# Between the scan and the experts: which engine copies the affinities out, who scales token tile eight, where the choice rounds stand, and 48 identity transposes

## The chip, the cores and the metric

The kernel runs on one core of one Trainium2 chip. The core has five engines that work in parallel, each through its own instruction list, and that wait for each other by semaphores: TensorE (PE, matmuls), VectorE (DVE), ScalarE (ACT), GpSimd (POOL) and SyncE (SP, which here only issues DMAs). The metric is the device time of one launch in microseconds (us), lower is better. One launch computes the whole model step for both inputs.

## The reference

Two inputs, a prompt of 256 tokens and a sample of 1024 tokens, of width 1024, go through one layer: a mixer (gated short convolution beside a bidirectional mLSTM) and a mixture of 16 experts in which each expert chooses its tokens. The part that matters here:

```python
def expert_choice_sublayer(x, norm_g, w_router, w_gate, w_up, w_down):
    n_tok = bsz * s
    cap = CAPACITY_FACTOR * n_tok // N_EXPERTS      # 128 for the sample, 32 for the prompt
    tokens = rms_norm(x, norm_g).reshape(n_tok, d)
    logits = jnp.einsum('nd,de->ne', tokens, w_router)
    affinity = jax.nn.softmax(logits, axis=-1)
    gate, idx = lax.top_k(affinity.T, cap)
    xe = tokens[idx]
    hid = jax.nn.silu(jnp.einsum('ecd,edf->ecf', xe, w_gate)) * jnp.einsum('ecd,edf->ecf', xe, w_up)
    ye = jnp.einsum('ecf,efd->ecd', hid, w_down) * gate[..., None]
    out = jnp.zeros((n_tok, d)).at[idx.reshape(-1)].add(ye.reshape(-1, d))
    return x + out.reshape(bsz, s, d)
```

So no expert can start before all affinities of a sequence are known, the top 128 of 1024 tokens have been found for each expert, and those tokens have been gathered.

## The kernel before

**The stages.** Tokens are cut into ten tiles of 128: tiles 0 to 7 are the sample (NS = 8), tiles 8 and 9 the prompt. The kernel first projects all tokens (to about 410 us), then runs a loop over the ten tiles (the scan with the output projection, the residual and the router), then chooses tokens, then runs 16 experts one after the other, then normalises and stores. Every engine's list is written out by hand in the source, so the order of the work on an engine is the order of the calls.

**The tile loop.** All engines run it with a counter n from 0 to NT + 1 = 11. Tile n's heads are computed at step n, its residual x1 (`residual`, L1307, in two halves of 512 columns) at step n + 1, and what is left of it at step n + 2, where m = n - 2 counts the tile: sum of squares (ACT, `token_squares`), router logits (PE, `logits`), softmax (`softmax_terms` on ACT, `affinities` on DVE). The normalised tokens go to DRAM as `tok_d`, from which the experts gather. For tiles 0 to 7 DVE makes them in one operation (`tokens_out`, L1436), and GpSimd issues the DMA. For the two prompt tiles ACT scales (L1042), GpSimd multiplies by the gain (L715) and issues the DMA (L718), after the loop. "Tile eight" in the list of changes is the last sample tile, m = 7.

**The choice.** `choose` (L1297) finds eight tokens a round for all experts together: a MAX8, a FIND_INDEX8 and a MATCH_REPLACE8 over 512 columns. There are 16 rounds, 0 to 15. AFF, the table that they search, is filled from PSUM: the sample's affinities in two copies by DVE (L1543) at step 9, the prompt's after round 11 (L1568). Rounds 0 to 5 lie between the work of the last steps of the loop, rounds 6 to 15 behind it. Then DVE computes the indices (`GIF`, L1584), PE transposes them (L1909), DVE writes `IDX` (L1593), and GpSimd starts two gathers: `xg` for the sample's rows (L743) and `xgp` for the prompt's quarter rows (L746). Both add to one semaphore, `gath`.

**The barrier.** Behind the loop SP, PE, ACT and GpSimd each do `barrier` (L341: `eng.drain().then_inc(bar)`, then wait for all five; DVE only arrives with `arrive` and waits for it before `IDX`). GpSimd first waits until all `acc_d` and `tok_d` writes have landed. Only behind the barrier does SP load expert weights: `load_weights` (L563), 1 MB at a time into `eraw`.

**The first expert.** ACT rounds five weight blocks (`high(0, 0, 0, j)` for j = 0 to 4, L1055, `ehi`), then the gathered tokens (`tokens_high`, L1066, `xc`) and then makes `xb` (`narrow_tokens`, L1061), in this order in its list. DVE makes the low parts (`elo`, `xc`). PE's `token_columns` (L1921) transposes the gathered rows; the expert's first matmul (L1928) waits for `xc`, `xb` and the first weights.

Of the kernel before, what the change touches and what calls it, by code (L numbers as in the profile page):

```python
# [6 lines left out]
ACT = mybir.ActivationFunctionType  # L7
# [6 lines left out]
P = 128  # L14
# [27 lines left out]
def hybrid_conv_mlstm_moe(nc, x_prompt, x_sample, norm1_g, w_in, conv_w, gate_bias, head_norm_g, w_out,  # L42
# [5 lines left out]
    NT = T // P  # L48
# [97 lines left out]
    with out:  # L146
# [157 lines left out]
        def final_tile(n):  # L304
# [18 lines left out]
            "x1_out0 x1_out1 sum2 tk_done tk_out0 tk_out1 xT_ps2 xT_done "  # L323
            "lg_ps lgmax exps aff_done affT_ps topk selT_ps sel_done "

            "er0 er1 er2 er3 er4 er5 er6 er7 ehi elo idx_cp gath exT_ps xc_hi xc_lo xb_done "
            "gu_ps gu_add sg_done hid_done hc_hi hc_lo hb_bf dn_ps y_done scat settled "

            "conv_done cvl_done g2b_in tk_scaled issued gf_in f_in0 f_in1 f_in2 f_in3 f_in4 f_sum f_y f_out f_gath f_same f_row f_sq f_quart f_done f_set").split()}
        x_in = (S["x_in0"], S["x_in1"], S["x_in2"])  # L330

        w_ind, stg = (S["w_in0"], S["w_in1"]), (S["st0"], S["st1"], S["st2"], S["st3"])
# [48 lines left out]
        def joint(m):  # L381

            return m >= NS


        def colslot(c, q):
# [217 lines left out]
        def _(pool):  # L604
# [94 lines left out]
            for n in range(NT + 2):  # L699
                if n >= 2:  # L700
                    m = n - 2
                    t = tokens_of(m)
                    pool.wait_ge(S["x1_done"], 2 * (m + 1))
                    pool.dma_start(acc_d[t, :], d["x1"][:, m % 2, :]).then_inc(x1_out[m % 2], 16)
                if 1 <= n < NT - 1:
                    scale_queries(n + 1)
                if 1 <= n < NT - 2:
                    select_causal(n + 2)
                if n >= 2 and not joint(m):
                    pool.wait_ge(S["tk_done"], m + 1)  # L710
                    pool.dma_start(tok_d[t, :], d["tk"][:, m % 2, :]).then_inc(tk_out[m % 2], 16)
            pool.wait_ge(S["g2b_in"], 16)
            for m in range(NS, NT):
                pool.wait_ge(S["tk_scaled"], m - NS + 1)
                pool.tensor_tensor(d["tk"][:, m % 2, :], d["tk"][:, m % 2, :], g2b, ALU.mult  # L715
                                   ).then_inc(S["tk_done"], 1)
                pool.wait_ge(S["tk_done"], m + 1)
                pool.dma_start(tok_d[tokens_of(m), :], d["tk"][:, m % 2, :]).then_inc(tk_out[m % 2], 16)  # L718
# [21 lines left out]
            def gather(idx):  # L740

                settle()
                pool.indirect_dma_start(f["xg"][:, :], None, tok_d,  # L743
                                        bass.IndirectOffsetOnAxis(ap=idx[:, 0:1], axis=0)
                                        ).then_inc(S["gath"], 16)
                pool.indirect_dma_start(f["xgp"][:, :], None, tok_quarters,  # L746
                                        bass.IndirectOffsetOnAxis(ap=idx[:, 1:2], axis=0)
                                        ).then_inc(S["gath"], 16)

            def scatter(e):  # L750

# [64 lines left out]
        def _(act):  # L816
# [165 lines left out]
            def token_squares(m):  # L982

                act.wait_ge(S["x1_done"], 2 * (m + 1))
                if m >= 1:
                    act.wait_ge(S["sum2"], m)
                act.activation(d["junk"][:, :], d["x1"][:, m % 2, :], ACT.Square, scale=D ** -0.5,
                               accum_out=d["ms"][:, m % 2, 0, H:H + 1]).then_inc(S["sum2"], 1)

            def softmax_terms(m):  # L990

                act.wait_ge(S["lgmax"], m + 1)
                act.activation(aff[:, m, :], psum[:, logit_bank(m), 0:NE], ACT.Exp, bias=logit_max[:, m, 0:1],
                               scale=d["ms"][:, m % 2, 1, H:H + 1],
                               accum_out=logit_max[:, m, 1:2]).then_inc(S["exps"], 1)
# [5 lines left out]
            for n in range(NT + 2):  # L1001
# [31 lines left out]
                    exponentials(n + 2)  # L1033
                if 1 <= n <= NT:
                    columns_out(n - 1, 0)
                if n < NT:
                    heads_high(n)
            for m in range(NS, NT):
                softmax_terms(m)
            for m in range(NS, NT):  # L1040
                act.wait_ge(tk_out[m % 2], 16 * (m // 2))
                act.activation(d["tk"][:, m % 2, :], d["x1"][:, m % 2, :], ACT.Copy, scale=d["ms"][:, m % 2, 1, H:H + 1]  # L1042
                               ).then_inc(S["tk_scaled"], 1)
            barrier(act, 1)

            def high(e, s, h3, j, first=False):
# [96 lines left out]
        def _(dve):  # L1143
# [162 lines left out]
            def residual(n, h):  # L1306
                dve.wait_ge(S["o_ps"], 2 * n + h + 1)  # L1307
                if h == 0:
                    dve.wait_ge(ld_x[n % 2], 16 * (n // 2 + 1))
                    if n >= 2:  # L1310
                        dve.wait_ge(x1_out[n % 2], 16 * (n // 2))
                        dve.wait_ge(S["tk_done"], n - 1)
                    else:

                        for q in range(NST):
                            dve.wait_ge(stg[q], 16 * len([g for g in staged if stage_no[g] % NST == q]))
                dve.tensor_tensor(d["x1"][:, n % 2, 512 * h:512 * h + 512], psum[:, 6 + h, :],
                                  d["xs"][:, n % 2, 512 * h:512 * h + 512], ALU.add).then_inc(S["x1_done"], 1)
# [197 lines left out]
            for n in range(NT + 2):  # L1516
                s, m = n % 2, n - 2
                if n == NT:
                    choose(both_halves, half, CAPS, 0, 2)
                if 1 <= n < NT:  # L1520
                    denominators(n)
                    if n == 1:
# [15 lines left out]
                    affinities(m)  # L1538
                if n == NT - 1:

                    dve.wait_ge(S["affT_ps"], 1)
                    for i in range(NS // 4):
                        ch(dve.tensor_copy(AFF[HALF2 * i:HALF2 * i + NE, :], psum[0:NE, (0, 4)[i], :]))  # L1543
                if n == NT:
                    logit_peak(m)
                    choose(both_halves, half, CAPS, 2, 4)
                if 2 <= n < NT - 1:
                    tokens_out(m)
                if 1 <= n <= NT:
                    residual(n - 1, 1)  # L1550
                if 1 <= n < NT:
                    heads_low(n)
                if n == NT - 1:
                    tokens_out(m)
                if n == NT + 1:
                    choose(both_halves, half, CAPS, 4, 5)
                    last_roots()
                    logit_bias(m - 1)
                    logit_peak(m)
                    logit_bias(m)  # L1560
                    choose(both_halves, half, CAPS, 5, 6)
                    affinities(m - 1)
                    affinities(m)

            arrive(dve)
            choose(both_halves, half, CAPS, 6, 12)
            dve.wait_ge(S["affT_ps"], 2)
            ch(dve.tensor_copy(AFF[PROMPT:SEL, 0:SP_], psum[0:NE, 1, 0:SP_]))  # L1568
            choose(slice(0, SEL), half, CAPS, 12, CAPS // 8)
# [121 lines left out]
        def _(pe):  # L1691
# [218 lines left out]
            pe.wait_ge(S["topk"], 2)  # L1910
            pe.transpose(psum[:, 4, 0:SEL], GV[:, :], ident[0:SEL, 0:SEL]).then_inc(S["selT_ps"], 1)

            def token_columns(e, g, bank):

                pe.wait_ge(S["gath"], 32 * e + 32)
                if bank == TOKEN_BANK:
                    pe.wait_ge(S["xc_lo"], 3 * e + g)
                rows = [f["xg"][:, k * P:(k + 1) * P] for k in range(4 * g, 4 * g + 4)] if g < 2 else \
                       [f["xgp"][:, c * P:(c + 1) * P] for c in range(2)]
                for k, x in enumerate(rows):  # L1920
                    tr = pe.transpose(psum[:, bank, k * P:(k + 1) * P], x, ident[:, :])  # L1921
                tr.then_inc(S["exT_ps"], 1)
# [128 lines left out]
```

## Time and profile before

| | us |
|---|---|
| median of three runs | 1375.62 |
| lowest and highest of the three | 1372.38, 1375.68 |
| the profiled execution, device time | 1374.1 |
| the profiled execution, first to last instruction (span) | 1372.4 |
| PE busy | 1276.9 (93%) |
| DVE busy | 916.6 (67%) |
| ACT busy | 706.2 (51%) |
| POOL busy | 310.5 (23%) |

The profile tells of one execution. Times in its rows count from the span's start. The stretch that the change touches runs from 560 to 660 us. In the page's 40 slices of 34.3 us PE is nearly full everywhere but in slices 18 and 19 (597 to 651 us or so), and there the clock granted to PE stands at 0.7 and 0.5 of full speed.

```profile
PE   4899999999998999943999999999999999999992
PEclk9999999999999999975999999999999999999996
```

### The profile page before, as it was taken

The page shows a single profiled execution, that of the slowest core. Times are in us where ns is not written, and L with a number is a line of the kernel's source. Part 1 is how long each engine was busy: PE and PEld are TensorE (multiplying, and loading weights), DVE is VectorE, ACT ScalarE, POOL GpSimd, SP SyncE. Part 2 cuts the span into 40 slices and gives each one's busy share as a digit, 9 for nine tenths or more (in the row PEclk, how much of TensorE's full clock was granted, in tenths as well). Part 3 has the DMA queues.
Part 4 walks back from the last instruction along what each step waited for, and adds up shares of the span by engine and source line. Part 5 has one row for each costly group of instructions (what it writes and reads, how often), then busy time and mean ns, then how long its engine had stood idle before and what let it go on. Part 6 is the DMA issues. An engine that isn't in the chain of part 4 may idle for free.

```text
span 1372.4 us, 24856 instructions
## 1 busy us (share of the span) xinstructions
PE 1276.9 (93%) x9696; PEld 1111.7 (81%) x9696; DVE 916.6 (67%) x1336; ACT 706.2 (51%) x1025; POOL 310.5 (23%) x304
## 2 busy tenths in 40 slices
PE   4899999999998999943999999999999999999992
PEld 4789999888887888832898889888898888888881
DVE  5345122251377555587888898888888898888976
ACT  5335321101145444314766677667766777666762
POOL 1032222010032232022123313132222313133040
PEclk9999999999999999975999999999999999999996
DMA  7113165314148765119799999999999999999994
GB/s 255 47 39 113 45 208 170 122 60 122 62 131 261 206 199 175 52 77 315 271 336 311 307 317 321 330 306 315 318 331 315 298 316 328 331 309 307 296 363 190
DMA packets 242030, 314.74 MB, mean 229 GB/s; under 512 B 16096, under 2 KB 206048, under 8 KB 241968
## 3 DMA queue, kind: packets, MB, share of 16 engines
q1 hardware_dynamic: 226576, 268.54, 59.4%
q0 software_dynamic: 15392, 45.36, 11.2%
q8 instruction: 41, 0.67, 0.2%
q14 instruction: 21, 0.17, 0.0%
HBM read 274.41 MB, written 39.44 MB: 229 GB/s over the span
## 4 chain that ended last, share of the span: by engine, by line
PE 89%; DVE 6%; DMA 2%; ACT 1%; issue 1%; SPq 0%; POOL 0%; DVEq 0%; ACTq 0%; POOLq 0%
PE psum L1851 25%; PE psum L1928 22%; PE psum L1935 10%; PE psum L1951 8%; PE psum L1743 7%; PE psum L1969 4%; PE psum L1960 4%; PE psum L1921 1%; PE psum L1789 1%; PE psum L1790 1%; PE psum L1776 1%; PE psum L1762 1%; DMA woraw<-in_w_out_dram 1%; PE psum L1724 1%; PE psum L1699 1%
## 5 line engine op out<-in xcount | busy, mean ns | idle before, releaser
L1602 DVE TENSOR_TENSOR elo<-eraw,ehi 128x2048 bf16<-128x2048 f32 x192 | 433.1, 2282 | 1.0 <-POOLq L761 1.0
L1055 ACT ACTIVATE ehi<-eraw 128x2048 fp32r<-128x2048 f32 x192 | 362.3, 1902 | 47.0 <-DMA eraw<-in_w_gate_dram 26.2
L1928 PE MATMUL psum<-xc,ehi 128*128 128x320 f32 x2048 | 332.4, 314 | 1.9 <-DVE xc L1607 1.9
L1928 PEld LDWEIGHTS psum<-xc,ehi 128*128 128x128 f32 x2048 | 304.2, 189 | 3.5 <-DVE xc L1607 2.3
L1935 PE MATMUL psum<-xb,elo 128*128 128x160 bf16 x2048 | 164.6, 234 | 0.0
L1615 DVE TENSOR_REDUCE gu<-psum 128x320 f32<-128x640 f32 x128 | 105.0, 820 | 85.1 <-PE psum L1935 84.9
L1935 PEld LDWEIGHTS psum<-xb,elo 128*128 128x128 bf16 x2048 | 139.3, 98 | 13.2 <-issue 0.2
L1851 PE MATMUL psum<-hn_hi,whi 128*128 128x512 f32 (+1 forms) x384 | 138.1, 360 | 5.8 <-DVE wlo L1179 5.8
L1851 PE MATMUL psum<-hn_lo,whi 128*128 128x512 f32 (+1 forms) x384 | 136.6, 356 | 0.0
L1851 PE MATMUL psum<-hn_hi,wlo 128*128 128x512 f32 (+1 forms) x384 | 136.5, 355 | 0.0
L1951 PE MATMUL psum<-ehi,hc 128*128 128x512 f32 x512 | 132.6, 406 | 0.0
L1951 PEld LDWEIGHTS psum<-ehi,hc 128*128 128x128 f32 x512 | 95.1, 188 | 22.2
L1106 ACT ACTIVATE sg<-gu 128x320 f32<-128x320 f32 x64 | 30.2, 472 | 145.1 <-DVE gu L1615 145.1
L1179 DVE SCALAR_TENSOR_TENSOR wlo<-wraw,g1c,whi 128x256 fp32r<-128x256 f32 x96 | 39.0, 477 | 95.2 <-ACT whi L838 95.1
L1851 PE MATMUL psum<-whi,hn_hi 128*128 128x256 f32 x320 | 91.6, 286 | 0.0
L1851 PE MATMUL psum<-wlo,hn_hi 128*128 128x256 f32 x320 | 90.5, 283 | 0.0
L1851 PE MATMUL psum<-whi,hn_lo 128*128 128x256 f32 x320 | 90.5, 283 | 0.0
L1851 PEld LDWEIGHTS psum<-hn_hi,whi 128*128 128x128 f32 x384 | 73.3, 191 | 16.6 <-DVE wlo L1179 6.0
L1851 PEld LDWEIGHTS psum<-hn_hi,wlo 128*128 128x128 f32 x384 | 73.2, 191 | 10.1
L1851 PEld LDWEIGHTS psum<-hn_lo,whi 128*128 128x128 f32 x384 | 73.3, 191 | 9.6
L754 POOL DMA_INDIRECT acc_d<-yt,idx x15 | 24.1, 1606 | 219.8 <-ACT yp L1076 219.8
L838 ACT ACTIVATE whi<-wraw,g1c 128x256 fp32r<-128x256 f32 x96 | 39.6, 497 | 53.5 <-PE psum L1851 51.5
(251 smaller groups left out, 1971.6 us busy)
## 6 DMA issues: line engine op xcount, KB each, us to landing
eraw<-in_w_gate_dram SPq DMA_DIRECT2D x64, 1024.0 KB, 9.6
eraw<-in_w_up_dram SPq DMA_DIRECT2D x64, 1024.0 KB, 9.9
eraw<-in_w_down_dram SPq DMA_DIRECT2D x64, 1024.0 KB, 13.9
wraw<-in_w_in_dram SPq DMA_DIRECT2D x12, 1024.0 KB, 7.6
negm<-negm_d SPq DMA_DIRECT2D x10, 512.0 KB, 7.4
acc_d<-x POOLq DMA_DIRECT2D x10, 512.0 KB, 5.4
tok_d<-tk POOLq DMA_DIRECT2D x10, 512.0 KB, 2.9
v<-v_d SPq DMA_DIRECT2D x18, 256.0 KB, 4.0
```

The source lines that it names most:

```text
L838: w = act.activation(b["whi"][:, j % 2, k, :], b["wraw"][:, j % 2, k, :], ACT.Copy, scale=b["g1c"][:, k:k + 1])
L1055: act.activation(f["ehi"][:, j % RING, :], f["eraw"][:, raw_slot(s, j), :], ACT.Copy).then_inc(S["ehi"], 1)
L1179: w = dve.scalar_tensor_tensor(b["wlo"][:, j % 2, k, :], b["wraw"][:, j % 2, k, :], b["g1c"][:, k:k + 1], b["whi"][:, j % 2, k, :].bitcast ...
L1602: dve.tensor_tensor(f["elo"][:, j % RING, :], f["eraw"][:, raw_slot(s, j), :], f["ehi"][:, j % RING, :].bitcast(F32), ALU.subtract).then_i ...
L1615: dve.tensor_reduce(f["gu"][:, (i // 2) % 2, i % 2, :, :], both, AX_X, ALU.add).then_inc(S["gu_add"], 1)
L1743: mm = pe.matmul(psum[:, 6 + h, :], x, w, start=(k == 0 and a == 0), stop=(k == KD - 1 and a == 2))
L1851: mm = pe.matmul(o, lhs, rhs, start=(k == 0 and a == 0), stop=(k == KD - 1 and a == 2))
L1928: pe.matmul(o[:, 0:2 * NC], hi[:, k, c], x[:, k, :, :].rearrange("p a t -> p (a t)"), start=(k == 0), stop=False, skip_group_check=True)
L1935: mm = pe.matmul(o[:, NC:2 * NC], lo[:, k, c], xb[:, k, :], start=False, stop=(k == KD - 1), skip_group_check=True)
L1951: mm = pe.matmul(psum[:, 4 + h, :], f["hc"][:, 2 * q + kk, a, :], f["ehi"][:, j % RING, full_columns(kk, h)], start=(q == 0 and kk == 0 an ...
L1960: pe.matmul(psum[:, 4 + h, :], f["hbf"][:, 2 * q + kk, :], f["elo"][:, j % RING, full_columns(kk, h)], start=False, stop=False, skip_group ...
L1969: mm = pe.matmul(psum[CAPP * i:CAPP * (i + 1), 6, 0:CH], f["hid"][:, k, CAPS:NC], f["eraw"][:, raw_slot(s, j), c], start=(k == 0), stop=(k ...
```

## The change

Six edits, all between tile step 9 and the first expert:

1. The sample's affinities are copied from PSUM into AFF by ACT (two ACTIVATE, behind `columns_out` of step 9), no more by DVE.
2. LATE = NS - 1 = 7: tile 7's tokens are treated as those of the prompt tiles. DVE's `tokens_out(7)` is gone; ACT scales the tile in step 9, behind `heads_high`, and GpSimd multiplies by the gain and issues the DMA behind the loop, so that it now does this for three tiles.
3. GpSimd waits for `aff_done` of all ten tiles before the first of these three multiplications.
4. The choice rounds are laid anew: round 0 stands in step 9 ahead of the second half of residual 8, round 1 at the head of step 10, rounds 2 to 4 behind the first half of residual 9, round 5 and 6 in step 11, and rounds 7 to 15 behind the loop.
5. The gather of the prompt's rows has a semaphore of its own, `gath_p`; PE's transposes of the sample's rows wait for `gath` alone.
6. PE does 48 transposes of the identity into a PSUM bank that nobody reads, between the transposes of the choice and those of the gathered tokens.

```diff
+        LATE = NS - 1
@@ GpSimd
-                if n >= 2 and not joint(m):
+                if n >= 2 and m < LATE:
                     pool.wait_ge(S["tk_done"], m + 1)
                     pool.dma_start(tok_d[t, :], d["tk"][:, m % 2, :]).then_inc(tk_out[m % 2], 16)
             pool.wait_ge(S["g2b_in"], 16)
-            for m in range(NS, NT):
-                pool.wait_ge(S["tk_scaled"], m - NS + 1)
+            pool.wait_ge(S["aff_done"], NT)
+            for m in range(LATE, NT):
+                pool.wait_ge(S["tk_scaled"], m - LATE + 1)
                 pool.tensor_tensor(d["tk"][:, m % 2, :], d["tk"][:, m % 2, :], g2b, ALU.mult
                                    ).then_inc(S["tk_done"], 1)
...
                 pool.indirect_dma_start(f["xgp"][:, :], None, tok_quarters,
                                         bass.IndirectOffsetOnAxis(ap=idx[:, 1:2], axis=0)
-                                        ).then_inc(S["gath"], 16)
+                                        ).then_inc(S["gath_p"], 16)
@@ ACT
+            def scaled_tokens(m):
+                act.wait_ge(tk_out[m % 2], 16 * (m // 2))
+                if not joint(m):
+                    act.wait_ge(S["lgmax"], m + 1)
+                act.activation(d["tk"][:, m % 2, :], d["x1"][:, m % 2, :], ACT.Copy, scale=d["ms"][:, m % 2, 1, H:H + 1]
+                               ).then_inc(S["tk_scaled"], 1)
...
+                if n == NT - 1:
+                    act.wait_ge(S["affT_ps"], 1)
+                    for i in range(NS // 4):
+                        act.activation(AFF[HALF2 * i:HALF2 * i + NE, :], psum[0:NE, (0, 4)[i], :], ACT.Copy
+                                       ).then_inc(S["aff_out"], 1)
                 if n < NT:
                     heads_high(n)
+                if n == NT - 1:
+                    scaled_tokens(LATE)
@@ DVE
-                        dve.wait_ge(S["tk_done"], n - 1)
+                        if n - 2 < LATE:
+                            dve.wait_ge(S["tk_done"], n - 1)
+                        else:
+                            dve.wait_ge(S["tk_scaled"], 1)
...
                 if n == NT:
-                    choose(both_halves, half, CAPS, 0, 2)
+                    choose(both_halves, half, CAPS, 1, 2)
...
-                    dve.wait_ge(S["affT_ps"], 1)
-                    for i in range(NS // 4):
-                        ch(dve.tensor_copy(AFF[HALF2 * i:HALF2 * i + NE, :], psum[0:NE, (0, 4)[i], :]))
+                    dve.wait_ge(S["aff_out"], NS // 4)
+                    choose(both_halves, half, CAPS, 0, 1)
                 if n == NT:
                     logit_peak(m)
-                    choose(both_halves, half, CAPS, 2, 4)
+                    choose(both_halves, half, CAPS, 2, 5)
...
-                if n == NT - 1:
-                    tokens_out(m)
                 if n == NT + 1:
-                    choose(both_halves, half, CAPS, 4, 5)
+                    choose(both_halves, half, CAPS, 5, 6)
...
-                    choose(both_halves, half, CAPS, 5, 6)
+                    choose(both_halves, half, CAPS, 6, 7)
...
-            choose(both_halves, half, CAPS, 6, 12)
+            choose(both_halves, half, CAPS, 7, 12)
@@ PE
+            for _ in range(48):
+                pe.transpose(psum[:, 2, 0:P], ident[:, :], ident[:, :])
...
-                pe.wait_ge(S["gath"], 32 * e + 32)
+                if g < 2:
+                    pe.wait_ge(S["gath"], 16 * e + 16)
+                else:
+                    pe.wait_ge(S["gath_p"], 16 * e + 16)
```

GpSimd's list at the end of the tile loop, from the last `tok_d` write inside the loop to the first gather. In the names `x` is a residual tile, `tk` a normalised tile, `og` the gain. Before:

```order
L711 DMA tok_d<-tk 128x1024 [waits s_tk_done]
L704 DMA acc_d<-x 128x1024 [waits s_x1_done] x2
L715 TENSOR_TENSOR tk<-tk,og 128x1024 [waits s_tk_scaled,s_g2b_in]
L718 DMA tok_d<-tk 128x1024 [waits s_tk_done]
L715 TENSOR_TENSOR tk<-tk,og 128x1024 [waits s_tk_scaled]
L718 DMA tok_d<-tk 128x1024 [waits s_tk_done]
L743 DMA xg<-tok_d,IDX 128x1024 [waits s_x1_out1,s_tk_out1,s_tk_out0,s_x1_out0,s_bar,s_sel_done]
```

Now:

```order
L706 DMA acc_d<-x 128x1024 [waits s_x1_done] x3
L718 TENSOR_TENSOR tk<-tk,og 128x1024 [waits s_tk_scaled,s_aff_done,s_g2b_in]
L721 DMA tok_d<-tk 128x1024 [waits s_tk_done]
L718 TENSOR_TENSOR tk<-tk,og 128x1024 [waits s_tk_scaled]
L721 DMA tok_d<-tk 128x1024 [waits s_tk_done]
L718 TENSOR_TENSOR tk<-tk,og 128x1024 [waits s_tk_scaled]
L721 DMA tok_d<-tk 128x1024 [waits s_tk_done]
L746 DMA xg<-tok_d,IDX 128x1024 [waits s_x1_out1,s_tk_out1,s_tk_out0,s_x1_out0,s_bar,s_sel_done]
```

One write of `tok_d` has moved behind the loop with a multiplication ahead of it, and the first multiplication has the added wait for `aff_done`. The number of DMAs is the same.

DVE's list in steps 9 and 10, from the affinities of tile 7 on (`GV`, `GI` and `AFF` rows are choice rounds). Before:

```order
L1426 TENSOR_SCALAR aff<-aff,logit_max 128x16 [waits s_dve_ch]
L1543 COPY AFF<-psum 16x512 [waits s_affT_ps]
L1543 COPY AFF<-psum 16x512 [waits s_dve_ch]
L1317 TENSOR_TENSOR x<-psum,xs 128x512 [waits s_o_ps,s_dve_ch]
L1404 TENSOR_TENSOR mxl<-psum,mxh 128x512 [waits s_mxh_done]
L1436 SCALAR_TENSOR_TENSOR tk<-x,ms,og 128x1024 [waits s_tk_out1]
L1301 MAX GV<-AFF 48x8
```

Now:

```order
L1446 TENSOR_SCALAR aff<-aff,logit_max 128x16 [waits s_dve_ch]
L1318 MAX GV<-AFF 48x8 [waits s_aff_out]
L1319 MAX_INDEX GI<-GV,AFF 48x8 [waits s_dve_ch]
L1321 MATCH_REPLACE AFF<-GV,AFF 48x512 [waits s_dve_ch]
L1337 TENSOR_TENSOR x<-psum,xs 128x512 [waits s_o_ps,s_dve_ch]
L1424 TENSOR_TENSOR mxl<-psum,mxh 128x512 [waits s_mxh_done]
L1318 MAX GV<-AFF 48x8
```

Two copies and the token scaling have left DVE, and a round stands ahead of the second half of residual 8.

ACT's list in the same place, from the copy of the first half of tile 8's columns (`xT`) on. Before:

```order
L979 ACTIVATE xT<-psum 128x512 [waits s_lg_ps,s_xT_ps2]
L971 ACTIVATE mxh<-psum 128x512 [waits s_mixT_ps]
L987 ACTIVATE junk,ms<-x 128x1024 [waits s_sum2,s_x1_done]
L979 ACTIVATE xT<-psum 128x512 [waits s_xT_ps2]
L979 ACTIVATE xT<-psum 128x512 [waits s_lg_ps,s_xT_ps2]
```

Now:

```order
L982 ACTIVATE xT<-psum 128x512 [waits s_lg_ps,s_xT_ps2]
L1051 ACTIVATE AFF<-psum 16x512 [waits s_affT_ps]
L1051 ACTIVATE AFF<-psum 16x512
L974 ACTIVATE mxh<-psum 128x512 [waits s_mixT_ps]
L998 ACTIVATE tk<-x,ms 128x1024 [waits s_lgmax,s_tk_out1]
L990 ACTIVATE junk,ms<-x 128x1024 [waits s_sum2,s_x1_done]
L982 ACTIVATE xT<-psum 128x512 [waits s_xT_ps2]
```

The scaling of tile 7 now stands ahead of the squares and the second column copy of tile 8.

## Rows read from the trace of the kernel before

**Rows 1.** The page: the chain that ended last, shares of the span by engine.

```profile
PE 89%; DVE 6%; DMA 2%; ACT 1%; issue 1%; SPq 0%; POOL 0%; DVEq 0%; ACTq 0%; POOLq 0%
```

**Rows 2.** Chain in order of time, from 631 us: start, length, what.

```profile
633.34 6.80 DMA xgp<-tok_d,IDX
```

**Rows 3.** Who waited for whom, SP's DMA queue: us in total, times, longest.

```profile
SPq L575 <- POOLq L343: 57.9, 1, 57.9
```

**Rows 4.** Line L343 (the barrier), then the kernel's end: duration in ns, start.

```profile
L343 POOLq DRAIN  x1: 9058/9058/9058, 611.3 to 611.3; - x1
...
L146 POOLq DRAIN  x1: 5437/5437/5437, 1366.7 to 1366.7; - x1
```

**Rows 5.** Groups by line, GpSimd's DMAs: busy us, mean ns, idle before.

```profile
L632 POOL DMA_DIRECT2D v_d<-stage x20 | 11.2, 562 | 45.0 <-ACT stage L870 45.0
...
L718 POOL DMA_DIRECT2D tok_d<-tk x2 | 1.2, 584 | 0.6 <-POOL tk L715 0.6
...
L756 POOL DMA_INDIRECT acc_d<-yp,idx x15 | 52.5, 3500 | 4.6 <-issue 4.6
...
L811 POOL DMA_INDIRECT out_y_prompt_dram<-yp,idx x1 | 1.0, 992 | 0.3 <-issue 0.3
```

**Rows 6.** Timeline of GpSimd: start, length, instruction, idle before and releaser.

```profile
602.37 2.34 POOL L715 TENSOR_TENSOR tk<-tk,og 128x1024 f32<-128x1024 f32 x1 [6.23 <-ACT tk L1042]
...
605.62 2.36 POOL L715 TENSOR_TENSOR tk<-tk,og 128x1024 f32<-128x1024 f32 x1
608.27 0.58 POOL L718 DMA_DIRECT2D tok_d<-tk  x1 [0.30 <-POOL tk L715]
```

**Rows 7.** Instructions that touch tile tk, 570 to 620 us: ns min/median/max.

```profile
L1042 ACT ACTIVATE tk<-x,ms x2: 1141/1141/1141, 601.1 to 602.1; 128x1024 f32<-128x1024 f32 x2
```

**Rows 8.** Timeline of SP's DMA queue: the first weight load.

```profile
620.42 0.38 SPq L575 DMA_DIRECT2D eraw<-in_w_gate_dram  x1
```

**Rows 9.** Timeline of ACT, from the first weight block to the first expert.

```profile
626.01 1.91 ACT L1055 ACTIVATE ehi<-eraw 128x2048 fp32r<-128x2048 f32 x1 [22.75 <-DMA eraw<-in_w_gate_dram]
...
639.29 1.91 ACT L1055 ACTIVATE ehi<-eraw 128x2048 fp32r<-128x2048 f32 x1 [2.38 <-DMA eraw<-in_w_gate_dram]
641.34 0.60 ACT L1066 ACTIVATE xc<-psum 128x512 fp32r<-128x512 f32 x1
...
643.10 1.27 ACT L1061 ACTIVATE xb<-xc 128x1280 bf16<-128x1280 f32 x1
```

**Rows 10.** Timeline of PE: transposes of gathered tokens, first expert's first matmuls.

```profile
640.18 1.97 PE L1921 MATMUL psum<-ident,xg 128*128 128x128 f32 x8 [9.25 <-DMA xgp<-tok_d,IDX]
...
644.46 4.60 PE L1928 MATMUL psum<-xc,ehi 128*128 128x320 f32 x16 [1.88 <-DVE xc L1607]
```

**Rows 11.** Windows of 1 us, PE: length, busy, granted clock, DMA share, GB/s.

```profile
599.00:600.00 1.00, 0.00 (x0) 0.62 0.05 16
...
650.00:651.00 1.00, 1.00 (x12) 0.78 1.05 418
```

**Rows 12.** Timeline of DVE, steps 9 to 11 of the loop and the choice.

```profile
577.05 1.39 DVE L1543 COPY AFF<-psum 16x512 f32<-16x512 f32 x2 [2.50 <-PE psum L1894]
...
588.69 0.69 DVE L1317 TENSOR_TENSOR x<-psum,xs 128x512 f32<-128x512 f32 x1 [1.46 <-PE psum L1743]
...
594.62 0.69 DVE L1317 TENSOR_TENSOR x<-psum,xs 128x512 f32<-128x512 f32 x1 [0.58 <-PE psum L1743]
...
603.02 1.72 DVE L1426 TENSOR_SCALAR aff<-aff,logit_max 128x16 f32<-128x16 f32 x1
...
604.85 0.23 DVE L1426 TENSOR_SCALAR aff<-aff,logit_max 128x16 f32<-128x16 f32 x1
...
614.38 0.69 DVE L1301 MAX8 GV<-AFF 48x8 f32<-48x512 f32 x1
...
616.67 0.69 DVE L1301 MAX8 GV<-AFF 48x8 f32<-48x512 f32 x1
...
630.00 0.28 DVE L1584 SCALAR_TENSOR_TENSOR GIF<-GIF,GI 16x128 f32<-16x128 f32 x1
```

More of the change, by code:

```diff
@@ L324, in hybrid_conv_mlstm_moe @@
             "lg_ps lgmax exps aff_done affT_ps topk selT_ps sel_done "
-            "er0 er1 er2 er3 er4 er5 er6 er7 ehi elo idx_cp gath exT_ps xc_hi xc_lo xb_done "
+            "er0 er1 er2 er3 er4 er5 er6 er7 ehi elo idx_cp gath gath_p exT_ps xc_hi xc_lo xb_done "
             "gu_ps gu_add sg_done hid_done hc_hi hc_lo hb_bf dn_ps y_done scat settled "
-            "conv_done cvl_done g2b_in tk_scaled issued gf_in f_in0 f_in1 f_in2 f_in3 f_in4 f_sum f_y f_out f_gath f_same f_row f_sq f_quart f_done f_set").split()}
+            "conv_done cvl_done aff_out g2b_in tk_scaled issued gf_in f_in0 f_in1 f_in2 f_in3 f_in4 f_sum f_y f_out f_gath f_same f_row f_sq f_quart f_done f_set").split()}
         x_in = (S["x_in0"], S["x_in1"], S["x_in2"])
@@ L1040, in _ @@
             for m in range(NS, NT):
-                act.wait_ge(tk_out[m % 2], 16 * (m // 2))
-                act.activation(d["tk"][:, m % 2, :], d["x1"][:, m % 2, :], ACT.Copy, scale=d["ms"][:, m % 2, 1, H:H + 1]
-                               ).then_inc(S["tk_scaled"], 1)
+                scaled_tokens(m)
             barrier(act, 1)
```

## The prediction

> **What bounds the kernel now.** I read first the page's chain by engine: PE holds 89% of it [rows 1], so an edit counts only where PE stands still. The page's slices show one such place that the change touches, between the scan and the first expert. There PE does no matmul of weight until 644.46 [rows 10], and its clock is down to half from about 599.6 to 650.5: the window of 599 to 600 us shows 0.62, the window of 650 to 651 shows 0.78 on the way up [rows 11]. Whatever moves the start of the first expert moves the end of the kernel by as much, since from there on PE is full.
>
> Two chains meet at that start, and the reader should hold them apart. The **choice chain** ends last in the profile: DVE ends the indices at 630.28 [rows 12], the gathers land at 633.34 + 6.80 = 640.14 [rows 2], PE transposes at 640.18 [rows 10], ACT copies at 641.34 [rows 9]. The **weight chain** is nearly as late and the chain view doesn't show it: SP waited 57.9 us for GpSimd's arrival at the barrier [rows 3] and began to load at 620.42 [rows 8]. The fifth block reached ACT at 639.29 and was rounded by 641.20 [rows 9]. Only then may ACT touch the gathered tokens, because the five blocks stand ahead of them in its list. So ACT went from weights to tokens within 0.14 us: the two chains tie. A gain on one alone is worth nothing, and a loss on the weight chain is paid in full.
>
> What sets the barrier is GpSimd: its last multiplication starts at 605.62, its last DMA is issued at 608.27 [rows 6], that DMA has landed when the drain begins at 611.3, and the drain itself takes 9.06 us [rows 4], to 620.36.
>
> **How long the drain will be.** The trace has a second drain of GpSimd, at the kernel's end, of 5.44 us [rows 4]. GpSimd's groups by line add up to 110 DMAs ahead of the first drain (v_d 20, o_d 20, state 20, qk 12, conv 12, rows 6, acc_d 10, tok_d 10) and 66 between the two (four indirect groups of 15 in the expert loop, and six single ones); the first and the last group of each are in [rows 5]. 9058 / 110 = 82.3 ns and 5437 / 66 = 82.4 ns: the drain goes with the number of DMAs since the last one. The change leaves that number at 110, so I take 9.06. The bounds: 5.44 from the other row, and nothing if the cost could be paid while GpSimd waits.
>
> **The change part by part.**
>
> *Copies by ACT (edit 1) and round 0 ahead of residual 8 (edit 4).* DVE loses 1.39 us of copies at 577.05 [rows 12]. ACT sits idle there and is no slower at it. A round takes 616.67 - 614.38 = 2.29 us [rows 12]. Round 0 ends at about 580.4 and holds the second half of residual 8 up by 0.5 us. That is covered by the next item.
>
> *Tile 7 scaled by ACT in step 9 (edit 2).* 1.14 us [rows 7] now stand on ACT ahead of tile 8's squares and of the column copy for which PE's logits wait. I price this at a PE delay of 1.1 us in steps 10 and 11 (0.5 if only DVE's delay counted). The first half of residual 9 goes from 588.69 to about 589.8.
>
> *Three rounds between the halves of residual 9 (edit 4).* From 589.8 DVE has 0.8 us (the residual and the logit peak, as between 588.69 and its next round), then 3 x 2.29 = 6.87. The second half starts at 597.46 where it was 594.62. From there to the end of the affinities it took 604.85 + 0.23 - 594.62 = 10.46 us [rows 12], with two rounds in it, as before. One of its pieces shrinks: the 16-column scaling took 1.72 us at 603.02 beside GpSimd's multiplication and 0.23 at 604.85 [rows 12]. With edit 3 the two never meet, which gives back 1.49. The affinities end at 597.46 + 8.97 = **606.4** in place of 605.1. Behind them stand nine rounds for ten, so the indices are ready at 630.3 + 1.35 - 2.29 = 629.3, **0.9 us earlier**. This is the gain that the change makes on the choice chain.
>
> *GpSimd waits for all affinities and has three tiles (edits 2 and 3).* Queued behind this wait are three multiplications, three `tok_d` writes, the drain and with it all weight loads. The tile cycle is 605.62 - 602.37 = 3.25 us [rows 6]. Starts: 606.5 and 609.7. The third can't start before ACT has scaled tile 9, and that now waits until tile 7's write has freed the buffer: issue at 606.5 + 2.65 = 609.1, 2.9 to land (the last write of before took 3.0 from issue to drain), 1.14 to scale, so 613.2 and not 613.0. Its DMA is issued at 613.2 + 2.65 = 615.85, the drain starts 3.0 later at 618.9 and ends at **627.9**. Before it was 620.36: **the barrier falls 7.55 us later**.
>
> The Trainium skill says in "SBUF — State Buffer", section "SBUF: two separate sides", that GpSimd and a DVE operation with two SBUF inputs lock a shared port pair against each other. By that rule the MATCH_REPLACE operations would stretch GpSimd's three multiplications by up to 0.7 us each, and the barrier would fall about 2 us later still. The trace speaks against it: the multiplication beside affinities took 2.34, the one beside choice rounds 2.36 [rows 6], so the sum keeps 2.35.
>
> *From barrier to first expert.* Weight loads start at 628.0. From the first load to the end of the fifth rounding it took 641.20 - 620.42 = 20.8 us [rows 8, 9], with the gathers in the same stretch as they will be now. So ACT is through at 648.75. From ACT's first token copy to the first matmul it took 644.46 - 641.34 = 3.12 us [rows 9, 10], of which about 0.3 was waiting for PE that is gone: start at **651.6**, 7.1 us later. The gathered rows are there long before, at about 639.2.
>
> *Gather signals split (edit 5).* Nothing: ACT isn't ready for tokens until 648.75. In the expert loop the gathers are hidden already.
>
> *48 identity transposes (edit 6).* Eight cold ones take 1.97 us [rows 10], so 48 take at most 11.8, from 629.7 to 641.5. They delay the real transposes by up to 2.3 us, under cover of ACT's weights. PE then has nothing from about 644 to 651.6, and the clock fell within about one microsecond of PE's last matmul before [rows 11]. So the first expert again starts at half clock. Before, it stayed there for 6 us of work, 644.46 to 650.5, and so lost 3 us. I take the same; with a rise after half that time it would be 1.5 less.
>
> **Sum.** 7.1 (start) + 0 (clock) = 7.1 us on the profiled execution's 1374.1: 1381.2. The median of the three runs is 1.5 above that execution; I forecast between the two bases, 1382. Unknown costs: PE delay in step 10 (-0.6), clock (-1.5 to +1), a late step of DVE or ACT (+1), base (-1 to +1).
>
> **Rivals.**
>
> *The drain is shorter.* If it costs 5.44 as at the end, the barrier falls at 624.3 and the start at 648.0, 3.5 later: 1378. Against it stand the two quotients of 82 ns.
>
> *The drain vanishes behind the added work, and the change does what it says (faster).* If what takes 9 us is done by the time that GpSimd has waited for the affinities and multiplied three tiles, the barrier falls at or before 620.4, the choice chain decides, and its 0.9 us count. So does the split signal, by up to 1 us (an estimate: half of the 1.97 us of the sample rows' transposes [rows 10] could stand ahead of the second gather's landing), and a clock at full from the start gives 3: 1374.1 - 4.9 = 1369, with the base 1370. The point from which it decides is a drain under 1.5 us. For it: the trace doesn't show what the drain does. Against it: both drains began only when nothing was left to land, and each still cost 82 ns for every DMA behind it. The Trainium skill, in "TensorE: Matmul & The Clock Gate", section "Part 4: PE-mode transpose", says that transposes don't engage the full clock; by that this rival would keep the 3 us of cold start and give 1373. No row here shows transposes alone for long enough to tell.
>
> *Slower still.* If GpSimd's multiplications are held up by DVE's rounds after all, or the cold stretch grows by the missing warm-up just ahead, 2 to 3 us more: 1385.
>
> **Chances.** Forecast 0.74 (own range 1379 to 1385), short drain 0.09, faster 0.08, slower still 0.09. The range 1377 to 1386 leaves out the fast rival, part of the short drain and a tail of the forecast, together under 2 in 10. A measurement of this kernel can tell about 0.3% (4 us) from no change: faster is below 1371.5, slower above 1379.7. Faster 0.08; within 0.17 (the short drain and 0.08 of the forecast's lower tail); slower 0.75.
>
> **What would show it.** In the profile of the changed kernel: GpSimd's drain near 9.06 us, beginning near 619; SP's first weight load near 628; affinities ended near 606.4 with no 1.72 us operation; the indices near 629.3; ACT idle until the first weight lands near 633.5 and going from the fifth block to tokens near 648.8 without a wait; the first expert's matmul near 651.6 at clock 0.5. The prediction is wrong if the drain is much under 9 us, if the first weight load is not later than 620, or if ACT waits for gathered tokens.

## The result and the profile after

| | before | changed |
|---|---|---|
| median of seven runs, us | 1375.55 | 1382.53 |
| lowest and highest | 1372.38, 1377.98 | 1381.29, 1384.0 |
| the profiled execution, device time | 1374.1 | 1382.53 |
| its span | 1372.4 | 1380.8 |

The ratio is 1.0059 with a 95% interval of 1.005 to 1.0069: the change makes the kernel 7 to 9.5 us slower. The profiled executions differ by 8.4 us.

The page's chain by engine, which answers to [rows 1], now has GpSimd's and SP's queues in it with a percent each:

```profile
PE 88%; DVE 4%; DMA 2%; ACT 2%; issue 1%; POOLq 1%; SPq 1%; POOL 0%; ACTq 0%; DVEq 0%
```

The chain in order of time (start, length, what) shows how. It leaves the choice and runs through GpSimd's tiles, its drain and the weight loads:

```profile
597.14 0.70 DVE x L1337
...
606.25 2.35 POOL tk L718
608.60 0.29 issue
608.89 2.96 DMA tok_d<-tk
611.85 0.02 issue
611.87 1.16 ACT tk L998
613.03 0.08 issue
613.11 2.33 POOL tk L718
...
615.74 2.95 DMA tok_d<-tk
...
618.80 9.07 POOLq L343
...
634.73 14.23 DMA eraw<-in_w_gate_dram
648.96 0.02 issue
648.98 1.91 ACT ehi L1072
650.89 1.25 ACT xc L1083 x3
652.14 0.02 issue
652.17 1.28 ACT xb L1078
653.45 0.09 issue
653.54 4.61 PE psum L1951 x16
```

One line after the other: the second half of residual 9 stands behind three choice rounds (597.14, where it was 594.62 in [rows 12]); GpSimd starts on tile 7 only at 606.25; tile 7's write must land before ACT may scale tile 9 into the same buffer; then the last write, the drain, and the weights. The drain has the very length of [rows 4], and so has the one at the end:

```profile
L343 POOLq DRAIN  x1: 9058/9058/9058, 618.8 to 618.8; - x1
...
L146 POOLq DRAIN  x1: 5437/5437/5437, 1375.1 to 1375.1; - x1
```

SP's first load, which answers to [rows 8]:

```profile
627.88 0.38 SPq L577 DMA_DIRECT2D eraw<-in_w_gate_dram  x1
```

ACT's timeline, which answers to [rows 9]:

```profile
633.68 1.91 ACT L1072 ACTIVATE ehi<-eraw 128x2048 fp32r<-128x2048 f32 x1 [20.66 <-DMA eraw<-in_w_gate_dram]
638.31 1.92 ACT L1072 ACTIVATE ehi<-eraw 128x2048 fp32r<-128x2048 f32 x1 [2.72 <-DMA eraw<-in_w_up_dram]
641.31 1.91 ACT L1072 ACTIVATE ehi<-eraw 128x2048 fp32r<-128x2048 f32 x1 [1.08 <-DMA eraw<-in_w_gate_dram]
644.33 1.91 ACT L1072 ACTIVATE ehi<-eraw 128x2048 fp32r<-128x2048 f32 x1 [1.12 <-DMA eraw<-in_w_up_dram]
648.98 1.91 ACT L1072 ACTIVATE ehi<-eraw 128x2048 fp32r<-128x2048 f32 x1 [2.74 <-DMA eraw<-in_w_gate_dram]
650.80 1.34 ACT L1083 ACTIVATE xc<-psum 128x512 fp32r<-128x512 f32 x3
```

A block comes every 3.0 us, but twice, at 638.31 and at 648.98, after 4.6. GpSimd's gathers (each brings one expert's token rows from DRAM) stand in both gaps: the first expert's issued from 630.74 on and, in the second gap, the second expert's:

```profile
639.29 0.19 POOL L740 COPY idx<-IDX 128x2 uint32<-128x2 uint32 x1 [6.25 <-PE psum L1944]
640.26 0.95 POOL L746 DMA_INDIRECT xg<-tok_d,idx  x1 [0.79 <-POOL idx L740]
```

PE, answering to [rows 10], and the granted clock in windows (length, busy, clock, DMA share, GB/s), answering to [rows 11]:

```profile
629.48 7.69 PE L1931 MATMUL psum<-ident 128*128 128x128 f32 x48
637.92 1.09 PE L1944 MATMUL psum<-ident,xg 128*128 128x128 f32 x8 [0.75 <-DMA xg<-tok_d,IDX]
...
653.54 4.61 PE L1951 MATMUL psum<-xc,ehi 128*128 128x320 f32 x16 [14.31 <-ACT xb L1078]
```

```profile
632.00:634.00 2.00, 2.00 (x12) 0.50 1.09 360
634.00:635.00 1.00, 1.00 (x10) 0.93 1.10 348
...
640.00:641.00 1.00, 0.00 (x0) 0.99 1.11 350
641.00:642.00 1.00, 0.00 (x0) 0.50 1.10 349
...
657.00:658.00 1.00, 1.00 (x6) 0.50 1.01 398
658.00:659.00 1.00, 1.00 (x16) 0.98 1.06 422
```

The identity transposes do bring the clock up, from 1.2 to 2.4 GHz near 634, and the eight transposes of gathered rows take 1.09 us for 1.97. But PE then waits 14.3 us for ACT, the clock is down again at 641, and the expert starts cold. DVE, answering to [rows 12]: the affinities end at 605.88 + 0.23 without a long operation, and the indices are 1.25 us earlier (0.96 if this execution's earlier loop, 0.29 us, is taken off).

```profile
605.55 0.23 DVE L1446 TENSOR_SCALAR aff<-aff,logit_max 128x16 f32<-128x16 f32 x1
...
605.88 0.23 DVE L1446 TENSOR_SCALAR aff<-aff,logit_max 128x16 f32<-128x16 f32 x1
...
628.75 0.28 DVE L1601 SCALAR_TENSOR_TENSOR GIF<-GIF,GI 16x128 f32<-16x128 f32 x1
```

### The profile page after: what moved, and what is told of

Read it like the earlier page. It is cut to its first block, busy times and chain, and to the rows that moved or that the text cites. A ratio compares the mean times of both kernels' runs of the same rounds, so it can differ in the third digit from the quotient of the medians.

```text
span 1380.8 us, 24954 instructions
## 1 busy us (share of the span) xinstructions
PE 1284.6 (93%) x9744; PEld 1119.5 (81%) x9744; DVE 912.5 (66%) x1333; ACT 708.2 (51%) x1028; POOL 307.4 (22%) x305
## 4 chain that ended last, share of the span: by engine, by line
PE 88%; DVE 4%; DMA 2%; ACT 2%; issue 1%; POOLq 1%; SPq 1%; POOL 0%; ACTq 0%; DVEq 0%
PE psum L1868 25%; PE psum L1951 22%; PE psum L1958 10%; PE psum L1974 8%; PE psum L1760 7%; PE psum L1992 4%; PE psum L1983 4%; PE psum L1806 1%; PE psum L1807 1%; PE psum L1944 1%; PE psum L1793 1%; DMA eraw<-in_w_gate_dram 1%; PE psum L1741 1%; POOLq L343 1%; DMA woraw<-in_w_out_dram 1%
## 5 line engine op out<-in xcount | busy, mean ns | idle before, releaser
L1951 PE MATMUL psum<-xc,ehi 128*128 128x320 f32 x2048 | 332.4, 314 | 14.3 <-ACT xb L1078 14.3
## 6 DMA issues: line engine op xcount, KB each, us to landing
eraw<-in_w_gate_dram SPq DMA_DIRECT2D x64, 1024.0 KB, 10.3
```

Source lines behind the costliest of these rows:

```text
L1951: pe.matmul(o[:, 0:2 * NC], hi[:, k, c], x[:, k, :, :].rearrange("p a t -> p (a t)"), start=(k == 0), stop=False, skip_group_check=True)
```

## The experiments

The theory: the loss is the later barrier, and the barrier is GpSimd's queue plus a drain that costs 82 ns for each DMA. Its rivals: the new order on DVE is the cost; the drain has a fixed cost; the rest of the change is worth something or nothing.

The tile loop begins its last steps at a time that varies by some 3 us between executions, so places are compared from a mark: r is the start of the first half of residual 8 on DVE, w the first weight load, s the first expert's first matmul, "rest" the span from s to the end. All from each kernel's profiled execution; medians against the runs of the kernel before on the same chip (their medians lay between 1374.6 and 1375.6). Where two kernels do the same work up to the barrier, w - r agrees to 0.05 us (a3, a4 and a5; b1 and b2; a10 and a12; changed and a6), so differences of some tenths in this column mean something. The column "rest" has the length of the cold stretch in it, which varies by itself, as told below.

| kernel | w - r | s - r | rest | median | ratio, 95% interval |
|---|---|---|---|---|---|
| before | 46.89 | 70.93 | 727.94 | 1375.55 | |
| changed | 54.64 | 80.30 | 727.26 | 1382.53 | 1.0059, 1.005 to 1.0069 |
| a1: tile 7 on DVE | 50.78 | 74.58 | 727.81 | 1378.35 | 1.0019, 1.0009 to 1.0029 |
| a2: no affinity wait | 50.21 | 74.06 | 726.55 | 1377.09 | 1.0023, 1.0014 to 1.0033 |
| a9: both undone | 49.78 | 73.81 | 727.29 | 1377.89 | 1.0023, 1.001 to 1.0036 |
| a6: second gather late | 54.62 | 78.53 | 727.83 | 1382.34 | 1.0057, 1.0044 to 1.0071 |
| a3: early drain | 46.04 | 69.50 | 727.12 | 1372.85 | 0.9988, 0.9978 to 0.9997 |
| a4: a3 without the 48 | 45.99 | 69.52 | 727.61 | 1372.85 | 0.9986, 0.9977 to 0.9995 |
| b1: before, early drain | 38.12 | 71.13 | 727.98 | 1374.67 | 0.9996, 0.9986 to 1.0005 |
| b2: before, both drains | 38.16 | 71.18 | 721.65 | 1369.02 | 0.996, 0.9947 to 0.9974 |
| a5: changed, both drains | 46.04 | 69.62 | 721.80 | 1367.03 | 0.9949, 0.9929 to 0.9969 |
| a10: a5, tile 7 on DVE | 41.88 | 67.74 | 721.34 | 1365.83 | 0.9941, 0.9926 to 0.9957 |
| a12: a10, warm to the start | 41.89 | 67.76 | 721.46 | 1365.03 | 0.9929, 0.9914 to 0.9944 |

**Which part moves the barrier (a1, a2, a9).** From the changed kernel, undone one at a time and together:

```diff
 a1: LATE = NS, DVE's tokens_out(7) back behind heads_low of step 9, no scaled_tokens(LATE)
 a2:
-            pool.wait_ge(S["aff_done"], NT)
 a9: both
```

> The changed kernel with one part undone: tile 7's tokens are made by DVE in step 9 again, so GpSimd multiplies two tiles behind the loop; its wait for the affinities stays. Theory (the later barrier is the cost, and it comes from GpSimd's queue): one cycle of 3.25 us less and about 0.8 us less delay of the affinities; the drain starts near 614.7 in place of 618.8 and still takes 9.06 us; first weight load near 623.8; time 4 us under the changed kernel, about 1378.5. Rival (the three choice rounds ahead of the second half of residual 9 are the cost): they stay, so the time stays within 1 us of 1382.5.

> The changed kernel without edit 3: GpSimd no longer waits for the affinities of all tiles before it multiplies tile 7. Theory (the barrier is what counts, and the wait puts three multiplications behind the affinities): tile 7 is multiplied near 598.7, right behind the last acc_d write, tile 8 near 604.8, tile 9 near 608; DVE's affinities stall behind tile 8's multiplication by about 1.3 us; the drain starts near 613.7, first weight load near 622.8, 5 us earlier than in the changed kernel, time about 1377. Rival (the wait pays, because DVE is what the start waits for): the DVE stall of 1.3 us shows in the time and it stays at 1382 to 1384.

> The changed kernel with edits 2 and 3 undone, so that GpSimd has the queue of the kernel before, with two tiles and without the wait; the copies on ACT, the new place of the rounds, the split gather signal and the 48 transposes stay. Theory (the whole loss is GpSimd's queue): tile 8 is multiplied near 604.5 and tile 9 right behind it, so the drain starts near 613.5 and the first weight load near 622.6, still 2 us later than before because the residual of tile 9 stands behind three rounds; time about 1376, 1 us above the kernel before. Rival (nothing but the GpSimd edits costs, and the rest gains its 0.9 us): 1374 or less.

a1 and a2 came out as the theory has it, 1378.35 and 1377.09. a9 was expected 1 us above the kernel before and is 3 above, by an interval of 1.4 to 4.9 us. Its ten times scatter more than the others', from 1374.5 to 1380.7 us; five lie below 1377 with a mean granted clock of 0.973 or 0.974, five above 1378.9 with 0.967 to 0.969, and its profile is one of the second five. What sets them apart is open. From the mark its first weight load is 2.9 us later than before: the second half of residual 9, which now stands behind three rounds, is 2.4 us later (23.52 for 21.09), and squares, roots, softmax and ACT's scaling of tile 8 follow it (30.46 for 27.55). That is the DVE rival's part, and it is real. From the column w - r the shift of 7.75 us then splits: 2.9 from what a9 keeps, above all the new order of the rounds, 0.4 more for tile 7 on GpSimd alone (a2), 1.0 more for the wait alone (a1), and with both another 3.4. The two edits cost little apart and much together. The copies on ACT, the places of the rounds and the split signal were not undone one by one. Without the wait tile 7 is multiplied while GpSimd has nothing to do:

```profile
598.24 2.36 POOL L717 TENSOR_TENSOR tk<-tk,og 128x1024 f32<-128x1024 f32 x1
...
604.97 2.34 POOL L717 TENSOR_TENSOR tk<-tk,og 128x1024 f32<-128x1024 f32 x1 [3.49 <-ACT tk L997]
```

These are a2's rows. The wait moves this work out of the gap and into the queue ahead of the drain. What the wait protects is small: in a2 one affinity scaling took 1.66 us beside a multiplication, for 0.23.

**What the drain costs (a3, b1, a5, b2).** One or two drains of GpSimd added where it idles; nothing else changes:

```diff
                     pool.dma_start(acc_d[t, :], d["x1"][:, m % 2, :]).then_inc(x1_out[m % 2], 16)
+                    if n == NT:
+                        pool.drain()
 a5, b2 also:
             i.then_inc(S["f_same"], 1)
+            pool.drain()
```

> The changed kernel with one operation added: GpSimd drains once in step 10 of the loop, in its idle time behind the acc_d write of tile 8. Theory (a drain costs 82.3 ns for each DMA since the last one): the early drain takes about 8.7 us (106 DMAs) in idle time, the one at the barrier about 0.3 us (4 DMAs); barrier near 619.3, first expert near 643, time about 1373, 9 us under the changed kernel. Rival (the drain has a fixed cost, or one that comes from the multiplications or transfers just ahead of it): the drain at the barrier stays near 9 us or keeps at least half of it, and the time stays within 4 us of 1382.5.

> The kernel before with the same early drain. Theory (weights and choice tie at the first expert in the kernel before): the barrier falls 8.5 us earlier, at about 612, but the choice chain still ends at 630.3 and the gathers at about 640, so the first expert moves by less than 1 us: 1375, no change that can be measured. Rival (the weight loads alone set the start before): about 8 us faster, 1367.

> As the kernel with the early drain, and a second drain added near the kernel's end, in the 32 us in which GpSimd waits for the last outputs. Theory: 64 of the 66 late DMAs are paid there (5.3 us, hidden), the last drain falls from 5.44 to about 0.2 us and the time by another 5.2 us, to about 1368. Rival (fixed cost): the last drain stays at 5.4 and the time at 1373.

> The kernel before with both added drains and nothing else. Theory: the early one gives nothing (the choice chain ends as late), the late one takes the last drain from 5.4 to 0.2 us: 1369.5, which leaves 2.5 to 3.5 us of the 9 us of the combined kernels to the edits of the change once the barrier is out of the way. Rival (the edits give nothing even then): 1367 or less.

Drains of the kernel a5 (early, barrier, late, end; ns, start):

```profile
L708 POOLq DRAIN  x1: 9295/9295/9295, 582.0 to 582.0; - x1
...
L343 POOLq DRAIN  x1: 381/381/381, 619.6 to 619.6; - x1
...
L808 POOLq DRAIN  x1: 5865/5865/5865, 1328.1 to 1328.1; - x1
...
L146 POOLq DRAIN  x1: 207/207/207, 1365.0 to 1365.0; - x1
```

The drains that began with nothing in flight took, by DMAs since the last drain: 2: 0.207 us, 3: 0.299 (b1), 4: 0.381, 66: 5.437, 110: 9.058. That is 0.05 plus 0.082 for each DMA, for direct and indirect ones alike. So the fixed-cost rival is out. The added drains began while a transfer was still in flight. They took 0.6 or 0.7 us more than this formula gives, and the late one of a10 2.2 more (7.47 us for 64 DMAs), all in idle time; why that one took longer is open. The four times that were expected of a3, b1, a5 and b2 were met within 1 us. b1 shows the tie of the kernel before: its barrier fell 8.8 us earlier and its first expert not at all, because ACT then waited 10.3 us for PE's transposes. Its five weight blocks came before any gather, every 3.0 us (617.38, 620.33, 623.36, 626.37, 629.37):

```profile
629.37 1.91 ACT L1057 ACTIVATE ehi<-eraw 128x2048 fp32r<-128x2048 f32 x1 [1.09 <-DMA eraw<-in_w_gate_dram]
641.59 0.60 ACT L1068 ACTIVATE xc<-psum 128x512 fp32r<-128x512 f32 x1 [10.31 <-PE psum L1923]
```

**Why the first expert was 9.1 us late and not 7.1 (a6).**

```diff
                     pool.wait_ge(S["exT_ps"], 3 * e + 3)
+                    if first:
+                        pool.wait_ge(S["ehi"], 5)
                     copy_indices(e + 1)
```

> The changed kernel with one wait added: GpSimd starts the gather for the second expert only when ACT has rounded the fifth weight block. Theory (the start was 9.1 us late and not 7.1 because that gather now falls between the first five weight blocks): the gap between the fourth and fifth block goes from 4.65 to about 3.0 us, the first expert starts near 651.9 in place of 653.5, and nothing is lost later, time about 1381. Rival (the blocks are slower for another reason, such as the gather of the first expert alone): the gap stays near 4.65 and the start where it is.

```profile
644.20 1.91 ACT L1074 ACTIVATE ehi<-eraw 128x2048 fp32r<-128x2048 f32 x1 [1.10 <-DMA eraw<-in_w_up_dram]
647.21 1.91 ACT L1074 ACTIVATE ehi<-eraw 128x2048 fp32r<-128x2048 f32 x1 [1.10 <-DMA eraw<-in_w_gate_dram]
```

The gap is 3.01 us and the first expert starts 1.77 earlier, as expected: the second gather was what stretched the fifth block. The gap of the first expert's gather stays (4.42 us). The time of 1381 was not met: the median is 1382.34, and against the kernel before no gain on the changed kernel is to be seen (1.0057 against 1.0059, intervals overlap). In the profile "rest" is 0.6 longer (727.83 for 727.26): the clock was back at 657.6, after 5.8 us of the expert, where the changed kernel had it back after 4.5.

**What the warm clock is worth (a4, a12), and all together (a10).** a4 is a3 without the 48 transposes. a10 is a5 with tile 7 on DVE. a12 adds to a10, behind PE's transposes of the gathered rows:

```diff
+            for _ in range(16):
+                pe.transpose(psum[:, 2, 0:P], ident[:, :], ident[:, :])
```

> The changed kernel with the early drain, without the 48 identity transposes. In the kernel with them the granted clock rose during them (0.93 in the window 634 to 635 us of the changed kernel), so they do warm it, but it had fallen again 1.8 us after PE's last transpose, and the first expert began at half clock. Theory: they buy nothing as long as PE then idles for 3.3 us; without them the start is at most 0.5 us later (cold transposes of the gathered rows) and the time about 1373, within 1 us. Rival (their warmth shortens the cold stretch of the first expert, 4.1 us with them against 6 us in the kernel before): about 1 us slower, 1374.

> All that helped, together: the changed kernel with tile 7 back on DVE, the early drain and the late drain. Theory: the barrier falls near 616.5 and the weight chain ends 3 us ahead of the gathers; ACT then waits for PE's transposes of the gathered rows, the first expert starts near 641.5, two microseconds after PE's last transpose, so the clock may still be full; time 1364 to 1365.5, 2 to 3 us under the kernel with both drains. Rival (the gathers land later when more weight blocks run beside them, or PE starts cold anyway): 1367, no gain on it.

> The kernel with tile 7 on DVE and both drains, with 16 more identity transposes between PE's transposes of the gathered rows and the first expert, to fill the 2 us in which PE waits for xc and xb. Theory (a warm-up counts only if it reaches the start): the clock stays at full through the start near 641.7; the cold stretch from 641.7 to 644.3 is gone, which saves 1.3 us: 1364.5. Rival (identity transposes don't hold the clock, or they hold up the start): the clock falls near 641.6 as before and the time is the same or worse, 1366.

a4's time is a3's, 1372.85 both, though from two chips (ratios 0.9986 and 0.9988): the 48 transposes buy nothing measurable where PE idles behind them. In the profiles "rest" differs by 0.5 us (727.61 without, 727.12 with). That is no more than the cold stretch varies anyway. From the first expert's start to the clock's return it lasted 6.0 us in the kernel before, 6.1 in b1, 5.4 in a4 and 3.8 in b2, all without the 48; with them 5.8 in a6, 5.7 in a1, 4.5 in the changed kernel, 4.3 in a3 and 3.0 in a2. a10 reached its start (67.7 from the mark, 1.9 us less than a5), but at a falling clock (1.00 in the window 640 to 641, 0.60 in the next). Its median of 1365.83 is just above the 1364 to 1365.5 that were expected and 1.2 below a5's, less than the intervals can tell apart. In a12 the clock stays at 1.00 in all windows from 638 us on and the first group of matmuls takes 2.58 us for 3.92. Yet "rest" is no shorter (721.46 for 721.34). PE, now faster, runs into the second expert's gather:

```profile
643.24 2.58 PE L1954 MATMUL psum<-xc,ehi 128*128 128x320 f32 x16 [0.32 <-issue]
...
651.29 0.66 PE L1947 MATMUL psum<-ident,xg 128*128 128x128 f32 x4 [0.83 <-DMA xg<-tok_d,idx]
```

Its median of 1365.03 is the lowest of all, 9.9 us under the kernel before, but over a10 no gain is shown.

b2, a5 and a10 also tell what the change is worth once the barrier is out of the way, for all three have both drains. The first expert starts 71.18 us from the mark in b2 (the kernel before), 69.62 in a5 (the changed one) and 67.74 in a10 (with tile 7 back on DVE): 1.6 and 3.4 us earlier. The ratios are 0.996, 0.9949 and 0.9941, in the same order, but their intervals overlap.

## Why the prediction was right

**The tie.** Right: b1 moved the weight chain alone and gained nothing, the change moved it the other way and paid in full.

**The affinities.** Forecast 606.4, measured 606.1; the mark itself lay 0.3 earlier in this execution than in the one before, so the working was met to 0.1 us.

One share of it was put in the wrong place. The prediction gave the delay of the first half of residual 9 (1.1 us; measured 16.22 from the mark for 15.16) to ACT's scaling of tile 7. In a1 and a9, where DVE makes tile 7 again, it still stands at 15.84: the scaling accounts for 0.4, and 0.7 stay with what these two kernels keep, round 0 in step 9 above all. The sum was right, in part by luck.

**GpSimd's queue.** Right to the step: multiplications at 606.25, 609.49 and 613.11 (forecast 606.5, 609.7, 613.2), the third one after ACT's late scaling; drain at 618.8 (618.9). The drain was argued from two quotients; a3, a5, b1 and b2 show it.

**The multiplications beside choice rounds.** They took 2.33, 2.35 and 2.33 us with MATCH_REPLACE operations beside them all along, so what the rival "slower still" said of a port is out for these operations. But they don't test the rule that the prediction used there, which is about operations with two inputs. Each such row in the trace (`MATCH_REPLACE8 AFF<-GV,AFF 48x512 f32<-48x512 f32`) has one input of 48x512, and a MATCH_VALUE_LOAD of 0.08 us brings the eight values ahead of it.

**From barrier to first expert.** This term was mis-sized: 23.0 us from the first load to the end of the fifth rounding, not 20.8. The step that failed is "with the gathers in the same stretch as they will be now". The first expert's gather was priced. The second expert's was not: it follows PE's transposes of the first rows, which now ended 9.7 us ahead of the start of the fifth rounding. In the kernel before they ended at 642.6, when the fifth block had been rounded, and its second gather came too late to stretch a gap. The rows are the fourth rounding on ACT and the gather on GpSimd, both of the kernel before:

```profile
635.00 1.91 ACT L1055 ACTIVATE ehi<-eraw 128x2048 fp32r<-128x2048 f32 x1 [1.10 <-DMA eraw<-in_w_up_dram]
...
643.62 0.95 POOL L743 DMA_INDIRECT xg<-tok_d,idx  x1 [0.79 <-POOL idx L737]
```

There only one gap was long, 4.29 us from 635.00 to 639.29. a6 shows the second gather's share, 1.6 of the 2.2 us. Of the other 0.6, the first gather's gap is 0.3 longer than before (4.63 for 4.29) and the first block comes 0.2 later after its load (5.80 for 5.59); why isn't shown. Start 653.54 for 651.6.

**The transposes of the identity.** They took 7.69 us and not up to 11.8, because the clock came up, and held nothing up: PE still waited 0.75 us for the gathered rows behind them.

**The clock.** Also mis-sized, the other way: it was cold from 653.54 to 658 and not for 6 us. "Rest" gives 0.7 us for it. No run ties this to the change, since a6 and a1 were cold for 5.8 and 5.7 us behind the same 48 transposes. The prediction's "within about one microsecond" for the fall of the clock held for the kernel before (last matmul ended at 598.7, 0.62 in the window from 599), but here it was down only 1.8 us after the last transpose. So 9.08 - 0.68 = 8.40 us, the difference of the spans; forecast 7.1. Against the medians the two sizes and the choice of the base cancelled, and 1382 for 1382.5 looks better than the working was: that part is luck.

**Rivals.** The short drain and the vanishing drain are out. The Trainium skill's sentence that transposes don't engage the full clock ("TensorE: Matmul & The Clock Gate", "Part 4: PE-mode transpose") is not borne out here: the clock rose to 0.93 in the window 634 to 635 us, with only transposes since 629.2. The forecast didn't hang on it.

## What to carry to other kernels

Where two chains tie, an edit that shortens one and lengthens the other by the same queue costs what it adds and gains nothing; look behind the chain view for the second one. Count everything that is queued behind an added wait, a drain included, and ask which idle time the wait keeps from being used. A drain of GpSimd can be paid early, where the engine idles: two added drains took 6 us off the kernel before, and 15 off the changed one.

## What the runs showed of the hardware

GpSimd's drain took 82 ns for each DMA that it had issued since its last drain, 0.2 us for 2 and 9.06 us for 110, though all had landed when it began. In the changed kernel PE's clock came up under transposes alone: they ran from 629.2, and the granted clock was 0.50 in the window 633 to 634 us and 0.93 in the next. It was down 1.8 us after PE's last transpose there, 0.6 us after PE's last matmul in the kernel before and 2.0 us after the last transpose in a2. A gather of 0.66 MB beside 1 MB weight loads stretched the way to the next block to 4.3 us in the kernel before and to 4.6 twice in the changed one, where blocks otherwise came every 3.0 us.
